# A hybrid encoder trunk with experts: the scatter of expert rows in column groups of the array

## The chip, the cores and the metric

The kernel runs on one core of a Trainium2 chip. Times are device microseconds (us) of one execution, and the median of several runs is compared. TensorE, VectorE, ScalarE, GpSimd and SyncE are the engines; SBUF is the working memory of 128 partitions, and PSUM is the memory that TensorE writes, eight banks of 128 partitions by 512 fp32 numbers. A matmul takes a stationary operand (loaded into the array by a weight load, up to 128 rows by 128 columns) and streams a moving operand of up to 512 columns through it; the stationary operand's columns become partitions of the result.

## What is computed

A trunk of two layers works on 256 tokens of width 1024. Each layer has a mixer (windowed attention beside a short convolution) and a feed-forward part: a dense SwiGLU in the first layer, and in the second a choice of 2 of 8 experts for each token. The reference, cut to the part around the change:

```python
def moe_swiglu(h, w_router, w_gate, w_up, w_down):
    t = h.reshape(b * s, d)
    logits = (t @ w_router).astype(jnp.float32)
    top_val, top_idx = lax.top_k(logits, TOP_K)
    gates = jax.nn.softmax(top_val, axis=-1)
    combine = jnp.sum(jax.nn.one_hot(top_idx, N_EXPERTS, dtype=jnp.float32) * gates[..., None], axis=1)
    out = jnp.zeros_like(t)
    for e in range(N_EXPERTS):
        out = out + combine[:, e:e + 1].astype(t.dtype) * swiglu(t, w_gate[e], w_up[e], w_down[e])
    return out.reshape(b, s, d)
```

## The kernel before

All weights come from HBM in fp32. ScalarE rounds a piece of 128 by 1024 weights to the matmul's fast fp32 format (line 425, `hi`), VectorE forms the rest (line 825, `lo`), and TensorE multiplies in three products, hi·hi, lo·hi and hi·lo (lines 1359 to 1361, `three`), each 128 by 512 columns. A ring of six pieces (`RING`) connects the three engines; the semaphore `lo_done` counts pieces that are ready, `piece_used` those that TensorE has finished. SyncE issues the weight transfers, each as soon as `lo_done` shows that its buffer is free.

In the expert layer TensorE runs `experts()` (line 1587). For each of the 8 experts in turn it works on a tile of up to 128 tokens: `gather` (line 1606) picks the expert's tokens from `xn` with a 0/1 matrix `sel`; `gu` computes gate and up in halves of 256 columns; `turn` transposes the gated rows; `down` accumulates the down projection in PSUM banks 3 and 4. The loop of `one_tile` (line 1639) does this for 14 halves. An expert with more than 128 tokens takes `two_tiles` (line 1665), with both tiles side by side. The plan for this (`code`) is computed on the chip, and here one expert of the eight, the last, takes two tiles.

The result of expert p−1 is added to the tokens while expert p has begun. ScalarE and VectorE copy banks 3 and 4 to `y`, 128 expert rows by 1024 (`rows_out`). `scatter_last` (line 1624) waits for both copies and for `gselT`, the 128-by-256 matrix that holds a row's gate weight at the column of its token, and calls `scatter` (line 1615). That makes four products: for each half t of the tokens and each half c of the width, `gselT` columns of t (128) are stationary and `y` columns of c (512) moving, all in plain fp32. Each lands in a bank of its own, 5, 6, 7 and 5 again; the last waits until the bank is free. Each product increments `scattered`, and VectorE then adds the bank to `x` (`add_rows`, line 1191; the addition is line 1199) and increments `x_changed`.

What follows on TensorE: in `one_tile` `clear` (line 1508) zeroes banks 3 and 4 with two matmuls of zeros, and `gu(1)` goes on with 24 matmuls, before `turn(0)` needs `gate(0)`, which VectorE does after the additions. In `two_tiles` the scatter is split (`r1=2`, `r0=2`, lines 1691 and 1693) around `gu_both`, and TensorE waits for all additions (`x_changed`, line 1696) before it clears. The second tile has a scatter of its own at line 1718, ahead of the next gather. A last scatter (line 1735) follows the loop; VectorE's additions, the final norm and the store come after it. Other places where TensorE uses less than the whole array are the scores of attention (line 1389), with 64 rows: heads 0 to 3 lie in rows 0 to 63 and heads 4 to 7 in rows 64 to 127. The router (line 1566) has a stationary operand of 16 columns.

Of the kernel before, what the change touches and what calls it, by code (L numbers as in the profile page):

```python
# [33 lines left out]
P = 128  # L34
# [60 lines left out]
def build_trunk(nc, x_d, pos_d, mix_g, w_in, conv_w, sink, att_g, conv_g, w_out, ffn_g, dg, du, dd,  # L95
                router, eg, eu, ed, final_g, out_d):
    ctx = ExitStack()
    with ctx:
        def sb(name, shape, dt=F32):
            return ctx.enter_context(nc.sbuf_tensor(name, shape, dt))  # L100
# [4 lines left out]
        bank = [ctx.enter_context(nc.psum_tensor(f"bank{i}", [P, 512], F32)) for i in range(8)]  # L105
# [14 lines left out]
        y = sb("y", [P, D])  # L120
# [5 lines left out]
        gselT = sb("gselT", [P, SEQ])  # L126
# [1211 lines left out]
        def _(pe):  # L1338
            mm, tr = nc.tensor.matmul, nc.tensor.transpose
# [247 lines left out]
            def experts():  # L1587
# [27 lines left out]
                def scatter(p, added, done, banks=(5, 6, 7, 5), r0=0, r1=4):  # L1615

                    for r in range(r0, r1):
                        t, c, b = r // 2, r % 2, banks[r]
                        if b in banks[:r]:
                            pe.wait_ge(added, p)  # L1620
                        mm(bank[b][:, :], gselT[:, t * P:(t + 1) * P], y[:, c * 512:(c + 1) * 512],  # L1621
                           start=True, stop=True).then_inc(done, 1)

                def scatter_last(p, banks=(5, 6, 7, 5), r0=0, r1=4):

                    if r0 == 0:
                        pe.wait_ge(y_act, p + 1)
                        pe.wait_ge(y_dve, p + 1)
                        pe.wait_ge(gselT_out, p + 1)
                    scatter(12 + 4 * p + 1, x_changed, scattered, banks, r0, r1)  # L1630
# [34 lines left out]
                def two_tiles(p, first, n0, u):  # L1665
# [50 lines left out]
                    pe.wait_ge(y2_dve, u + 1)  # L1716
                    pe.wait_ge(gselT2_out, u + 1)
                    scatter(4 * u + 1, x_changed2, scattered2, (0, 1, 2, 7))
                    gather(p + 2)
                    pe.wait_ge(x_changed2, 4 * u + 4)  # L1720
# [43 lines left out]
```

## Time and profile before

| what | value |
|---|---|
| median of 3 runs | 1656.64 us (1655.93 to 1657.57) |
| span of the profiled execution, first to last instruction | 1653.7 us |
| its total with what lies around the span | not given; the median is 2.9 us above the span |
| TensorE, matmuls | busy 1590.2 us, 96% |
| TensorE, weight loads (beside the matmuls) | busy 1306.2 us, 79% |
| VectorE | busy 1177.2 us, 71% |
| ScalarE | busy 986.1 us, 60% |
| mean granted TensorE clock | 0.987 |

In the profile PE is TensorE's matmuls, PEld its weight loads, DVE VectorE, ACT ScalarE. A duration of a matmul is its latency: successive matmuls overlap, so a stream is read by the distance of its starts. In a timeline row the columns are the start in us from the span's start, the time to the end of the group in us, engine, line, operation, operands (output <- inputs), the stationary operand's rows*columns, the moving operand's partitions by columns, and the number of instructions (x). What stands in brackets is the idle time ahead and who ended it. The granted clock is a share of 2.4 GHz.

### The profile page before, as it was taken

The page shows a single profiled execution, that of the slowest core. Times are in us where ns is not written, and L with a number is a line of the kernel's source. Part 1 is how long each engine was busy: PE and PEld are TensorE (multiplying, and loading weights), DVE is VectorE, ACT ScalarE, POOL GpSimd, SP SyncE. Part 2 cuts the span into 40 slices and gives each one's busy share as a digit, 9 for nine tenths or more (in the row PEclk, how much of TensorE's full clock was granted, in tenths as well). Part 3 has the DMA queues.
Part 4 walks back from the last instruction along what each step waited for, and adds up shares of the span by engine and source line. Part 5 has one row for each costly group of instructions (what it writes and reads, how often), then busy time and mean ns, then how long its engine had stood idle before and what let it go on. Part 6 is the DMA issues. An engine that isn't in the chain of part 4 may idle for free.

```text
span 1653.7 us, 22917 instructions
## 1 busy us (share of the span) xinstructions
PE 1590.2 (96%) x7170; PEld 1306.2 (79%) x7170; DVE 1177.2 (71%) x1467; ACT 986.1 (60%) x1335; POOL 9.8 (1%) x33
## 2 busy tenths in 40 slices
PE   7989999898799999999999999999999998999996
PEld 6777888787678878878878878878887887788874
DVE  5754545557589799789979979979979974645443
ACT  6544434454467587677767767767767753434342
POOL 2000000000000000000000000000000000000000
PEclk9999999999899999999999999999999999999999
DMA  9344463320779979979979979979988992644500
GB/s 346 125 154 153 180 225 119 138 102 2 267 298 382 351 269 382 351 270 389 344 267 388 347 268 393 341 289 373 385 307 309 383 350 92 237 152 155 194 6 26
DMA packets 177794, 417.89 MB, mean 253 GB/s; under 512 B 4144, under 2 KB 8272, under 8 KB 177760
## 3 DMA queue, kind: packets, MB, share of 16 engines
q1 hardware_dynamic: 176400, 415.25, 67.5%
q0 software_dynamic: 512, 1.12, 0.2%
q10 hardware_dynamic: 848, 1.06, 0.2%
q8 instruction: 22, 0.36, 0.1%
q14 instruction: 12, 0.10, 0.0%
HBM read 416.36 MB, written 1.05 MB: 252 GB/s over the span
## 4 chain that ended last, share of the span: by engine, by line
PE 90%; DVE 6%; ACT 3%; issue 1%; DMA 0%; DVEq 0%; ACTq 0%
PE bank L1359 27%; PE bank L1361 26%; PE bank L1360 26%; PE bank L1611 5%; PE bank L1621 2%; DVE lo L825 1%; PE bank L1599 1%; ACT raw_d L485 1%; ACT act_hi L425 1%; DVE mx L914 1%; DVE raw_d L911 1%; PE bank L1468 0%; PE bank L1409 0%; DVE act_lo L849 0%; PE bank L1680 0%
## 5 line engine op out<-in xcount | busy, mean ns | idle before, releaser
L825 DVE TENSOR_TENSOR lo<-raw_gu,hi 128x1024 fp32r<-128x1024 f32 x544 | 631.3, 1220 | 34.3 <-ACT hi L425 32.8
L1359 PE MATMUL bank<-hi,act_hi 128*128 128x512 f32 (+1 forms) x1408 | 559.2, 397 | 18.2 <-DVE lo L825 6.6
L425 ACT ACTIVATE hi<-raw_gu 128x1024 fp32r (+1 forms) x544 | 542.9, 1055 | 43.7 <-PE bank L1361 32.5
L1361 PE MATMUL bank<-hi,act_lo 128*128 128x512 f32 (+1 forms) x1408 | 548.4, 390 | 0.0
L1360 PE MATMUL bank<-lo,act_hi 128*128 128x512 f32 (+1 forms) x1408 | 548.4, 389 | 0.0
L825 DVE TENSOR_TENSOR lo<-raw_d,hi 128x1024 fp32r<-128x1024 f32 x246 | 290.5, 1223 | 57.4 <-ACT hi L425 56.8
L1359 PEld LDWEIGHTS bank<-hi,act_hi 128*128 128x128 f32 x1408 | 266.4, 189 | 74.1 <-issue 13.6
L1361 PEld LDWEIGHTS bank<-hi,act_lo 128*128 128x128 f32 x1408 | 266.2, 189 | 55.5
L1360 PEld LDWEIGHTS bank<-lo,act_hi 128*128 128x128 f32 x1408 | 266.9, 190 | 50.9
L425 ACT ACTIVATE hi<-raw_d 128x1024 fp32r (+1 forms) x246 | 247.0, 1056 | 0.0
L1359 PE MATMUL bank<-hi,at_hi 128*128 128x512 f32 x592 | 232.4, 393 | 11.4 <-DVE lo L825 5.9
L1361 PE MATMUL bank<-hi,at_lo 128*128 128x512 f32 x592 | 231.0, 390 | 0.0
L1360 PE MATMUL bank<-lo,at_hi 128*128 128x512 f32 x592 | 230.4, 389 | 0.0
L425 ACT ACTIVATE at_hi<-bank 128x256 fp32r<-128x256 f32 (+1 forms) x123 | 52.8, 429 | 229.7 <-PE bank L1599 191.3
L1359 PEld LDWEIGHTS bank<-hi,at_hi 128*128 128x128 f32 x592 | 111.1, 188 | 37.9 <-DVE lo L825 8.8
L1361 PEld LDWEIGHTS bank<-hi,at_lo 128*128 128x128 f32 x592 | 111.1, 188 | 23.4
L1360 PEld LDWEIGHTS bank<-lo,at_hi 128*128 128x128 f32 x592 | 111.2, 188 | 22.6
L1244 DVE TENSOR_TENSOR gated<-silu,bank 128x256 f32<-128x256 f32 x28 | 10.5, 418 | 109.5 <-ACT silu L707 109.5
L1611 PE MATMUL bank<-sel,xn 128*128 128x128 f32 x320 | 77.7, 404 | 1.1 <-DVE sel L1156 1.1
L1611 PEld LDWEIGHTS bank<-sel,xn 128*128 128x128 f32 x320 | 77.0, 334 | 1.5 <-issue 1.4
L707 ACT ACTIVATE silu<-bank 128x256 f32<-128x256 f32 x28 | 9.2, 382 | 111.4 <-PE bank L1361 111.4
L1177 DVE TENSOR_TENSOR at_lo<-bank,at_hi 128x256 fp32r<-128x256 f32 x98 | 41.6, 424 | 42.9 <-ACT at_hi L425 39.4
(202 smaller groups left out, 727.7 us busy)
## 6 DMA issues: line engine op xcount, KB each, us to landing
raw_gu<-in_moe_w_gate SPq DMA_DIRECT2D x56, 2048.0 KB, 9.4
raw_gu<-in_moe_w_up SPq DMA_DIRECT2D x56, 2048.0 KB, 14.2
raw_d<-in_moe_w_down SPq DMA_DIRECT2D x56, 2048.0 KB, 16.3
raw_gu<-in_w_in SPq DMA_DIRECT2D x7, 2048.0 KB, 13.1
raw_gu<-in_dense_w_gate SPq DMA_DIRECT2D x5, 2048.0 KB, 8.0
raw_gu<-in_dense_w_up SPq DMA_DIRECT2D x5, 2048.0 KB, 12.9
raw_d<-in_dense_w_down SPq DMA_DIRECT2D x5, 2048.0 KB, 15.4
raw_gu<-in_w_out SPq DMA_DIRECT2D x8, 1024.0 KB, 9.6
```

The lines of the kernel that those rows point to most:

```text
L425: return nc.scalar.activation(out, in_, ACT.Copy, **kw)
L485: nc.scalar.activation(prob[:, h * 256:(h + 1) * 256], prob[:, h * 256:(h + 1) * 256], ACT.Exp, bias=nmx[:, t, h:h + 1], accum_out=psums[: ...
L825: v.tensor_tensor(out, src, h, ALU.subtract).then_inc(lo_done, 1)
L911: link(v.scalar_tensor_tensor(out=two_heads, in0=bank[b][:, :].rearrange("p (h n) -> p h n", h=2), scalar=HD ** -0.5, in1=mask[:, t, :].un ...
L914: ins = v.tensor_reduce(mx[:, 2 * b:2 * b + 2], two_heads, AX, ALU.max)
L1177: v.tensor_tensor(at_lo[:, c], bank[2][:, c], at_hi[:, c], ALU.subtract).then_inc(atTl_done, 1)
L1359: mm(out, ah, wh, start=start, stop=False, **kw)
L1360: mm(out, ah, wl, start=False, stop=False, **kw)
L1361: return mm(out, al, wh, start=False, stop=stop, **kw)
L1599: ins = tr(bank[2][:, c:c + P], gated[:, half, i * P:(i + 1) * P], ident[:, :])
L1611: ins = mm(bank[5 + k // 4][:, (k % 4) * P:(k % 4 + 1) * P], xn[:, t, k:D:KT], sel[:, t, :], start=t == 0, stop=t == 1)
L1621: mm(bank[b][:, :], gselT[:, t * P:(t + 1) * P], y[:, c * 512:(c + 1) * 512], start=True, stop=True).then_inc(done, 1)
```

## The change

`scatter` issues each product in parts: for t = 0 two matmuls with 64 stationary columns each, written to partitions 0 to 63 and 64 to 127 of the bank; for t = 1 four with 32 columns each, written to four quarters of the partitions. All parts of a product stream the same 512 columns of `y`. The increment is on the last part. The callers, waits and semaphore counts stay.

```diff
--- before.py
+++ after.py
@@ -1618,8 +1618,12 @@
                         t, c, b = r // 2, r % 2, banks[r]
                         if b in banks[:r]:
                             pe.wait_ge(added, p)
-                        mm(bank[b][:, :], gselT[:, t * P:(t + 1) * P], y[:, c * 512:(c + 1) * 512],
-                           start=True, stop=True).then_inc(done, 1)
+                        wide = 64 if t == 0 else 32
+                        for g in range(P // wide):
+                            m = slice(g * wide, (g + 1) * wide)
+                            ins = mm(bank[b][m, :], gselT[:, t * P + g * wide:t * P + (g + 1) * wide],
+                                     y[:, c * 512:(c + 1) * 512], start=True, stop=True)
+                        ins.then_inc(done, 1)
 
                 def scatter_last(p, banks=(5, 6, 7, 5), r0=0, r1=4):
 
```

## Rows read from the trace of the kernel before

**Rows 1.** The page: span, engines, the chain that ended last.

```profile
span 1653.7 us, 22917 instructions
...
PE 1590.2 (96%) x7170; PEld 1306.2 (79%) x7170; DVE 1177.2 (71%) x1467; ACT 986.1 (60%) x1335; POOL 9.8 (1%) x33
...
PE 90%; DVE 6%; ACT 3%; issue 1%; DMA 0%; DVEq 0%; ACTq 0%
...
PE bank L1359 27%; PE bank L1361 26%; PE bank L1360 26%; PE bank L1611 5%; PE bank L1621 2%; DVE lo L825 1%; PE bank L1599 1%; ACT raw_d L485 1%; ACT act_hi L425 1%; DVE mx L914 1%; DVE raw_d L911 1%; PE bank L1468 0%; PE bank L1409 0%; DVE act_lo L849 0%; PE bank L1680 0%
```

**Rows 2.** Windows over three expert periods: length, PE, PEld, DVE, ACT, POOL busy, clock.

```profile
830.90:961.60 130.70, 129.86 (x578) 106.63 (x578) 112.56 (x125) 94.97 (x118) 0.00 (x0) 1.00 0.90 336
...
1092.30:1223.00 130.70, 129.86 (x578) 106.63 (x578) 112.57 (x125) 94.98 (x118) 0.00 (x0) 1.00 0.90 337
```

**Rows 3.** The chain in one period, longest pieces: start, us, what.

```profile
961.60 7.63 PE bank L1611 x32
...
981.78 3.43 PE bank L1621 x8
```

**Rows 4.** Timeline, first scatter: start, us, engine, line, operation.

```profile
458.56 0.39 PE L1361 MATMUL bank<-hi,act_lo 128*128 128x512 f32 x1
458.79 3.59 PE L1621 MATMUL bank<-y,gselT 128*128 128x512 f32 x8
461.82 1.03 PE L1511 MATMUL bank<-zeros 128*128 128x512 f32 x2
462.68 0.39 PE L1359 MATMUL bank<-hi,act_hi 128*128 128x512 f32 x1
...
460.93 0.19 PEld L1621 LDWEIGHTS bank<-y,gselT 128*128 128x128 f32 x1 [0.24 <-issue]
```

**Rows 5.** Line 1621: durations in ns (min/median/max), first and last start.

```profile
L1621 PE MATMUL bank<-y,gselT x80: 590/592/1193, 458.8 to 1645.6; 128*128 128x512 f32 x80
```

**Rows 6.** Timeline, two-tile expert: the split scatter and the clear behind it.

```profile
1390.55 1.88 PE L1621 MATMUL bank<-y,gselT 128*128 128x512 f32 x4
...
1404.68 1.88 PE L1621 MATMUL bank<-y,gselT 128*128 128x512 f32 x4
...
1407.65 0.98 PE L1511 MATMUL bank<-zeros 128*128 128x512 f32 x3 [0.66 <-DVE x L1199]
```

**Rows 7.** Timeline, the second tile's scatter and the last; window with the clock.

```profile
1626.41 3.67 PE L1621 MATMUL bank<-y,gselT 128*128 128x512 f32 x8 [0.83 <-ACT y L425]
...
1641.13 5.09 PE L1621 MATMUL bank<-y,gselT 128*128 128x512 f32 x8 [3.34 <-DVE y L1189]
...
1641.13:1643.80 2.67, 2.67 (x3) 0.50 0.00 0
```

**Rows 8.** Timeline, attention scores on 64 rows and neighbours; their durations in ns.

```profile
47.90 0.39 PE L1361 MATMUL bank<-hi,act_lo 128*128 128x512 f32 x1
48.22 2.96 PE L1389 MATMUL bank<-raw_d 64*128 64x256 f32 x16
51.11 0.50 PE L1359 MATMUL bank<-hi,act_hi 128*128 128x512 f32 x1
...
51.45 0.40 PE L1360 MATMUL bank<-lo,act_hi 128*128 128x512 f32 x1
...
50.37 0.81 PE L1389 MATMUL bank<-raw_d 64*128 64x256 f32 x3
...
373.19 1.10 PE L1389 MATMUL bank<-raw_d 64*128 64x256 f32 x4 [0.41 <-DVE raw_d L928]
...
L1389 PE MATMUL bank<-raw_d x64: 376/376/480, 48.2 to 375.8; 64*128 64x256 f32 x64
```

**Rows 9.** Timeline, weight loads of the values product, and durations of line 1409.

```profile
389.84 3.65 PEld L1409 LDWEIGHTS bank<-raw_d 128*128 128x128 f32 x32
...
L1409 PEld LDWEIGHTS bank<-raw_d x128: 186/192/192, 74.9 to 393.3; 128*128 128x128 f32 x128
```

**Rows 10.** Line 1566 (router), weight loads of 16 columns.

```profile
L1566 PEld LDWEIGHTS bank<-act_hi,rout_hl x8: 92/93/93, 429.5 to 432.1; 128*16 128x16 f32 x8
```

## The prediction

> **What bounds the kernel now.** I began with the page. TensorE is busy 96% of the span and carries 90% of the chain that ended last; line 1621, the scatter that is edited, has 2% of that chain [rows 1]. The next question was whether the experts, where the line runs, are as full as the average. Three expert periods of 130.70 us each, cut at the gather, show TensorE busy for 129.86 us in every one, at full clock, with VectorE at 112.57 us and ScalarE at 94.98 us [rows 2]. So TensorE is the bound there, and a microsecond added to its queue is a microsecond of the kernel unless it falls into the 0.84 us a period that TensorE is idle. The chain of such a period has the gather and the scatter as its longest pieces, the scatter's 3.43 us in full [rows 3].
>
> Then the scatter itself. One fp32 matmul of the program is two matmul instructions in the trace: 4 calls are x8, 3.43 us, 0.429 us each, with weight loads of 0.19 us beside them that never delay one; the matmuls before and after follow without a gap [rows 4]. Ten scatters make the x80 of the line [rows 5]: seven in the one-tile experts (first and last at 458.95 and 1243.18), one in the two-tile expert, split by `r1=2` and `r0=2` into two fours with gate and up pieces between [rows 6], one more for its second tile, behind an idle of 0.83 us, and the last of all, which follows an idle of 3.34 us and takes 5.09 us, with a granted clock of 0.50, the lower level of 1.2 GHz, over its first 2.67 us [rows 7].
>
> **The change.** It keeps what is computed and takes the 128 token columns of a call as 2 groups of 64 (t = 0) or 4 groups of 32 (t = 1). Each group streams the same 512 columns of `y`. Of 40 calls, 20 become 2 and 20 become 4: 80 matmul instructions become 20·2·2 + 20·4·2 = 240, and as many weight loads. No wait, DMA or semaphore count changes; the increment sits on the last group's matmul, so VectorE's additions (line 1199) are released at a call's end as now. What decides is what 240 instructions cost on the array. There are three terms.
>
> *Streaming.* If groups run side by side, a call still lasts two slots of 0.429 us and the term is 0. If they run one behind the other, it is 160 extra instructions at 0.429 us = 68.6 us. Line 1621 can't say which, but the attention scores can: they use 64 rows of the array, heads 0 to 3 the lower, heads 4 to 7 the upper half. A lone stream of them has its starts 0.217 us apart ((0.81 − 0.376) / 2, 376 ns being the duration of one) [rows 8]. Sixteen in one line would last 15·0.217 + 0.10 (the late second start, below) + 0.376 = 3.73 us; the row says 2.96 [rows 8]. Four slots less 0.1 are missing, so two streams did run at once, at full rate each. Those are row halves, not column groups, but it is the nearest row there is, and I take 0, with 68.6 as the other end.
>
> *Switching the split.* The last whole-array matmul starts at 47.90, the first half-array one at 48.22, 0.32 us later where 0.23 is the rule; another time the first four take 1.10 us to the fourth's end, so the second came 1.10 − 0.376 − 2·0.217 = 0.29 us behind the first, where 0.217 is the rule. On the way back 50.81 (last start, 50.37 + 2·0.217) to 51.11 is 0.30 for 0.217, and 51.11 to 51.45 is 0.34 for 0.23 [rows 8]. Each switch thus costs 0.09 us before its first matmul and about 0.1 behind it: 0.19. I read it as the array running empty and then waiting for a weight load that is hidden otherwise. The edit makes three switches in a scatter (128 to 64, 64 to 32, 32 to 128), four where it is split in two, and only one that counts in the last (64 to 32). 7·3 + 4 + 3 + 1 = 29 switches, 5.5 us. Bounds: 0, should column groups need no emptying, and 29·0.2 = 5.8.
>
> *Getting the groups started.* The second group of 64 can start only when three loads are in (its own is the third), the fourth of 32 when seven are; the groups end staggered by as much, and the next split waits for the last. That is 2 and 6 loads more than the first needs. Where loads are the limit (the 128-by-64 products of attention, 32 in 3.65 us) one of 128 columns comes every 0.112 us [rows 9]. Scaled by width, 0.056 and 0.028, it is 2·0.056 + 6·0.028 = 0.28 us a scatter; 16-column loads took 93 ns where 128-column ones took 186 to 192, so width does matter [rows 9, 10]. Against it, a narrower first load exposes 0.06 and 0.08 less than the 0.1 above. Net 0.14, times ten: 1.4 us. Bounds: −1.3 (no stagger), and with loads at 0.112 whatever their width 9 us, plus 8·0.112 − 0.857 = 0.04 for each of 20 calls: 10 us.
>
> What hides nothing: ScalarE and VectorE get the delay as slack, as TensorE hardly waits for them here; the additions of the one-tile case have the 24 matmuls of `gu(1)` behind them, 24·0.227 = 5.4 us, before `gate(0)` is wanted. In the two-tile case TensorE already waits 0.66 us for the addition at line 1199 before it clears [rows 6]; a later scatter moves that wait, it does not absorb it. Behind the last scatter stand only additions, the final norm and the store, all in line. The expert DMAs are prefetched against `lo_done` and see nothing.
>
> The sum is 0 + 5.5 + 1.4 = 6.9 us. The profiled span of 1653.7 us becomes 1660.6. The page gives no total for that execution; the median of the runs, 1656.64, lies 2.9 us above its span, and I carry the difference: **1663.6 us**, with an own range of 1660 to 1672 from the bounds of the second and third terms.
>
> **A rule weighed against the trace.** By FIFO, the scores above would save one slot only, where head 4 follows head 3, and their row would read 3.5 us, not 2.96 [rows 8]; so matmuls of the upper half must have begun ahead of earlier ones of the lower. The Trainium skill (TensorE: Matmul & The Clock Gate, "Part 3: Packing small matmuls — row/col tiling") says that matmuls keep program order in start and end without exception. By that rule, the trace disagrees, and the sum would be that of the second rival. The same section measured three column tiles at 2.38 times one's rate, which speaks against the third rival; no row here shows column groups.
>
> **Rivals.**
> 1. *Not slower.* Column groups share the rows through which `y` streams, so the change of width may need no emptying, and the queue runs through all three widths without a step. Then only the stagger is left, between −1.3 and +2.8 us with the narrow loads, and the kernel lies at 1655.5 to 1659.5, likeliest 1656.6. It decides if a switch costs under 0.07 us, since 29 of them are then 2 us. Against it: the switch of the scores costs 0.19 on the way in and on the way back [rows 8]. Chance 0.13.
> 2. *Groups start in program order.* Each group is a pair (high part, low part) that must follow itself, so its second instruction pairs only with the next group's first. Two calls of two groups are 8 instructions in 5 slots for 4, two of four groups 16 in 9 for 4: six slots of 0.429, 2.6 us a scatter, 25.7 us in all. With the switches 1656.6 + 25.7 + 5.5 = 1688. For it: a fixed order is the simplest machine. Against it: rows 8, as far as halves of rows speak for groups of columns. Chance 0.12.
> 3. *The change does not do what it says.* The narrow operands are run with the array whole, or the groups queue for the one stream of `y`, which row halves do not share (each half reads its own partitions, here all four groups read the same ones). 68.6 us, with or without switches: 1725 to 1731. Chance 0.10.
>
> **How the numbers follow.** The forecast (side by side, switches paid) has 0.62, a remainder of 0.03 goes to what I don't see. About 0.2%, 3.3 us, is what a measurement of this kernel can tell from no change; the forecast's range begins at 3.4, so nearly all of it is slower, and rival 1 is "same". Faster 0.03, same 0.13, slower 0.84. The range takes the forecast, rival 1 and rival 2 and leaves rival 3 and the remainder out: 1656 to 1689.
>
> **What would show it.** In the changed profile line 1621 has x240 matmuls. If the forecast holds, the one-tile scatter takes some 4.1 us from its first matmul to the clear for 3.43 now, the clear comes about 0.3 us behind the last group's start where 0.43 would be a slot, four starts of a 32-wide call fall within about 0.2 us, and the expert period grows from 130.70 to about 131.4 us. A period of 133.9 is rival 2, one of 138 rival 3, one of 130.7 to 130.9 rival 1. I am wrong if starts of different groups stand a full 0.429 us apart, if the loads come more slowly than 0.1 us each, or if the period grows by more than the scatter does, as that would be an engine I took to have slack.

## The result and the profile after

The changed kernel took 1663.01 us (median of 4 runs, 1661.44 to 1663.58), the kernel before 1656.29 us beside it (4 runs, 1655.27 to 1657.57): a ratio of 1.0040, 95% interval 1.0027 to 1.0052, 6.7 us more. 1663.6 had been forecast. The profiled execution is the one of 1661.44 us, with a span of 1659.7 us, 6.0 us over that of before. The total is close, and the way to it is not the one predicted, so the profile after is read in some detail.

From the page after, the lines that answer to [rows 1]:

```profile
span 1659.7 us, 23237 instructions
PE 1596.8 (96%) x7330; PEld 1299.0 (78%) x7330; DVE 1177.5 (71%) x1467; ACT 985.8 (59%) x1335; POOL 9.8 (1%) x33
```

160 more matmuls and as many loads, as counted. Busy time of the matmuls grows by 6.6 us only, since groups that run side by side are not counted twice. Line 1621 is now line 1624; its entry (durations in ns, first and last start, forms) gives:

```profile
L1624 PEld LDWEIGHTS bank<-y,gselT x240: 106/110/231, 458.8 to 1651.2; 128*32 128x32 f32 x80, 128*64 128x64 f32 x40
L1624 PE MATMUL bank<-y,gselT x240: 592/592/1061, 458.8 to 1651.6; 128*32 128x512 f32 x80, 128*64 128x512 f32 x40
```

The count is x240; the forms at the end list only a part of it. A matmul of a narrow group has the same median of 592 ns as one of the whole array [rows 5]. The timeline of the first scatter, matmuls:

```profile
458.51 0.39 PE L1361 MATMUL bank<-hi,act_lo 128*128 128x512 f32 x1
458.83 3.79 PE L1624 MATMUL bank<-y,gselT 128*64 128x512 f32 x24
462.55 0.73 PE L1511 MATMUL bank<-zeros 128*128 128x512 f32 x2
463.12 0.40 PE L1359 MATMUL bank<-hi,act_hi 128*128 128x512 f32 x1
```

and the loads of the same stretch:

```profile
458.83 0.20 PEld L1624 LDWEIGHTS bank<-y,gselT 128*64 128x64 f32 x4 [0.35 <-issue]
459.31 0.14 PEld L1624 LDWEIGHTS bank<-y,gselT 128*64 128x64 f32 x2 [0.29 <-issue]
459.74 0.14 PEld L1624 LDWEIGHTS bank<-y,gselT 128*64 128x64 f32 x2 [0.29 <-issue]
460.69 0.16 PEld L1624 LDWEIGHTS bank<-y,gselT 128*32 128x32 f32 x8 [0.81 <-issue]
461.15 0.13 PEld L1624 LDWEIGHTS bank<-y,gselT 128*32 128x32 f32 x4 [0.30 <-issue]
461.58 0.13 PEld L1624 LDWEIGHTS bank<-y,gselT 128*32 128x32 f32 x4 [0.30 <-issue]
462.55 0.30 PEld L1511 LDWEIGHTS bank<-zeros 128*128 128x128 f32 x2 [0.84 <-issue]
```

Two matmuls stand in the first slot, by a narrower window of the same timeline:

```profile
458.83 0.65 PE L1624 MATMUL bank<-y,gselT 128*64 128x512 f32 x2
```

The loads tell the order best (an fp32 matmul of the program is two instructions, a high and a low part, each with its load). At 458.83 four loads go out within 0.2 us (two groups, two parts each), then two at a time every 0.43 us; at 460.69 eight within 0.16 us, which is one load's 0.11 and 0.05 more, then four at a time every 0.43 us. So all groups of a call run together, slot by slot. The changes of width are the gaps: from the last whole-array product to the first group, 458.51 to 458.83, it is 0.32 us where 0.23 is the distance without a change. The 64-wide slots of 0.43 us begin at 458.83, 459.31 (0.05 late: the load of this slot is exposed, which means that TensorE waits for it) and 459.74, the fourth by that at 460.17, to end at 460.60; the 32-wide loads come at 460.69, 0.09 late. From the last product ahead to the first behind the clear it is 4.61 us (458.51 to 463.12), where it was 4.12 (458.56 to 462.68 [rows 4]): **0.49 us a scatter**, for 0.71 forecast.

The expert period, though, grew by more. These are the scatter's pieces in the chain that ended last, in the kernel after, one period apart each:

```profile
590.36 3.72 PE bank L1624 x24
721.78 3.72 PE bank L1624 x24
853.23 3.72 PE bank L1624 x24
```

131.42 and 131.45 us, and 131.42 to 131.46 over all six, for 130.70: 0.74 more, so 0.25 us a period lies outside the scatter. Nearly all of it (0.24) is in the loop over the halves of an expert. The transposes at line 1599 end each half of an iteration; before, then after:

```profile
535.46 0.38 PE L1599 MATMUL bank<-ident,gated 128*128 128x128 f32 x2
...
569.12 0.38 PE L1599 MATMUL bank<-ident,gated 128*128 128x128 f32 x2
```

```profile
536.05 0.38 PE L1599 MATMUL bank<-ident,gated 128*128 128x128 f32 x2
...
569.78 0.38 PE L1599 MATMUL bank<-ident,gated 128*128 128x128 f32 x2
```

Two iterations take 33.66 us before and 33.73 after: 16.83 and 16.87 each, six an expert, 0.24 us. The loss sits in the first ten or so products behind the transposes: nine distances in a row take 2.09 us (544.93 to 547.02) where they took 2.06 (544.33 to 546.39), and the later ones in the half keep their 0.227. No engine is waited for there.

The two-tile expert lost nothing. Its lines after, for [rows 6]:

```profile
1395.85 1.94 PE L1624 MATMUL bank<-y,gselT 128*64 128x512 f32 x8
1410.01 1.92 PE L1624 MATMUL bank<-y,gselT 128*32 128x512 f32 x16
1411.87 0.66 PE L1684 MATMUL bank<-ident,gated 128*128 128x128 f32 x4
1412.89 1.20 PE L1511 MATMUL bank<-zeros 128*128 128x512 f32 x4 [0.36 <-DVE x L1199]
```

From the first half scatter to the clear it is 17.04 us for 17.10. The first half is followed by a wait for VectorE's gates (line 1244), which shrank from 1.26 to 1.11 us. Behind the second half, TensorE's wait for VectorE's additions shrank from 0.66 to 0.36 us, because VectorE's own work ahead of them sets their time: its timeline in the kernel after shows that it begins its gates 5.24 us later than before (1410.89 for 1405.65), as far as everything had slid by then, and adds right behind them:

```profile
1410.89 0.75 DVE L1244 TENSOR_TENSOR gated<-silu,bank 128x256 f32<-128x256 f32 x2 [8.26 <-ACT silu L707]
1411.56 1.28 DVE L1199 TENSOR_TENSOR x<-x,bank 128x512 f32<-128x512 f32 x2
```

The last two scatters, for [rows 7]:

```profile
1631.62 3.79 PE L1624 MATMUL bank<-y,gselT 128*64 128x512 f32 x24 [0.83 <-ACT y L425]
1635.34 7.89 PE L1611 MATMUL bank<-sel,xn 128*128 128x128 f32 x32
1643.07 0.38 PE L1640 MATMUL bank<-ident,gsel 128*128 128x128 f32 x2
1646.78 5.43 PE L1624 MATMUL bank<-y,gselT 128*64 128x512 f32 x24 [3.34 <-DVE y L1189]
```

Behind the first of these stands the gather (line 1611). Its first two matmuls, before and then after:

```profile
1629.92 0.51 PE L1611 MATMUL bank<-sel,xn 128*128 128x128 f32 x2
```

```profile
1635.34 0.74 PE L1611 MATMUL bank<-sel,xn 128*128 128x128 f32 x2
```

The second starts 0.23 us later than it did, and the gather as a whole takes 7.73 us to the transposes behind it for 7.49. So nearly all of the 0.24 us stands at this one place, and it fits a load that the change back to 128 columns exposes: the load at 1635.34 begins with the gather's first matmul and takes 0.31 us, where before the loads ran ahead. Those at lines 1511 and 1359 take 0.19, so that more is exposed here.

The last scatter takes 5.43 us for 5.09, but this is not the price of its one change of width. It comes behind an idle and runs in good part at the lower granted clock (0.50 over its first 2.67 us before [rows 7], 0.57 over its first 3.99 us after), and the moments when the clock falls and rises differ from run to run. The scatter that no edit touched takes 5.09 us in the profile before, 5.12 in e7, 5.26 in e6 and 5.37 in e11 and e12 (kernels of the next section); the changed one takes 5.43 here and 6.68 in e10, where the granted clock is 0.50 over the first 5.97 us of it.

The account of the 6.0 us of the span, by starts in the two traces: seven one-tile scatters 3.4; the loops and what lies between, up to the two-tile expert, 1.9; the two-tile expert −0.1; the second tile's scatter, and the gather behind it, 0.4; the last scatter 0.3, clock included. Each is rounded.

### The profile page after: what moved, and what is told of

It is laid out like the page before. It is cut to its first block, busy times and chain, and to the rows that moved or that the text cites. A ratio compares the mean times of both kernels' runs of the same rounds, so it can differ in the third digit from the quotient of the medians.

```text
span 1659.7 us, 23237 instructions
## 1 busy us (share of the span) xinstructions
PE 1596.8 (96%) x7330; PEld 1299.0 (78%) x7330; DVE 1177.5 (71%) x1467; ACT 985.8 (59%) x1335; POOL 9.8 (1%) x33
## 4 chain that ended last, share of the span: by engine, by line
PE 90%; DVE 6%; ACT 3%; issue 1%; DMA 0%; DVEq 0%; ACTq 0%
PE bank L1359 27%; PE bank L1361 26%; PE bank L1360 26%; PE bank L1611 5%; PE bank L1624 2%; DVE lo L825 1%; PE bank L1599 1%; ACT raw_d L485 1%; ACT act_hi L425 1%; DVE mx L914 1%; DVE raw_d L911 1%; PE bank L1468 0%; PE bank L1409 0%; DVE act_lo L849 0%; PE bank L1511 0%
```

## The experiments

The views used are the same in all: the distance of the scatters in the chain (period), the timeline from the last product ahead of the scatter to the first behind the clear (scatter), and the distance of the transposes (loop, the time of one iteration, two halves). All numbers are of the one-tile experts. "over before" is against 4.12 us for the scatter.

| kernel | scatter over before, us | period, us | loop, us | ratio to before, 95% |
|---|---|---|---|---|
| before | 0 | 130.70 | 16.83 | |
| the change (64, 64, 32, 32) | 0.49 | 131.44 | 16.87 | 1.0040 (1.0027 to 1.0052) |
| e1 all 64 | 0.35 | 131.30 | 16.87 | 1.0043 (1.0026 to 1.0060) |
| e2 all 32 | 0.34 | 131.06 | 16.83 | 1.0014 (1.0005 to 1.0024) |
| e3 alternating | 0.78 | 131.50 | 16.83 | 1.0045 (1.0029 to 1.0062) |
| e4 one group | 7.33 | 138.07 | 16.83 | one run, 1730.6 us |
| e5 group first | 1.37 | 132.13 | 16.83 | one run, 1669.7 us |
| e6 before, delayed | 0.46 | 131.17 | 16.83 | one run, 1659.4 us |
| e7 before, dead code | 0 | 130.70 | 16.83 | 0.9998 (0.9988 to 1.0007) |
| e8 change, dead code | 0.49 | 131.45 | 16.87 | 1.0033 (1.0020 to 1.0045) |
| e9 change, delayed 0.46 | 0.95 | 131.90 | 16.87 | one run, 1666.2 us |
| e10 change, delayed 0.23 | 0.72 | 131.67 | 16.87 | one run, 1666.7 us |
| e11 before, delayed 0.35 | 0.35 | 131.07 | 16.83 | one run, 1658.5 us |
| e12 before, delayed 0.49 | 0.49 | 131.33 | 16.83 | one run, 1661.2 us |

Where a period has grown by more than scatter and six loops account for (0.14 us in e12), the rest lies in the products between the clear and the first transposes. Single periods agree to 0.05 us, kernel totals to a microsecond or more: the first scatter of these traces starts anywhere from 458.2 to 461.2 us, whatever the kernel, and the last takes more or less of the lower clock, so a difference of totals is only read where several runs stand behind it. (That is why e10's 1666.7 us stand over e9's 1666.2, with periods 0.23 us shorter.)

### What the width costs: e1, e2, e3

```diff
-                        wide = 64 if t == 0 else 32
+                        wide = 64                          # e1
+                        wide = 32                          # e2
+                        wide = 64 if c == 0 else 32        # e3
```

> All four products of a scatter in two groups of 64. The change's own scatter took 0.49 us more than the one before, from the last matmul ahead of it to the second clear, and its period 131.43 us for 130.70. Theory (groups run side by side, only changes of width cost, 0.09 us to run empty plus the exposed load: 0.05 for 64 columns, 0.03 for 32, 0.11 for 128): two changes of width, 0.09 + 0.05 + 0.09 + 0.11 + 0.01 for the second group's start = 0.35 us a scatter over before, period 130.70 + 0.35 = 131.05, or 131.29 if the 0.24 us a period that the change shows outside its scatter come again. Rival (groups take part of each other's time, by number of groups): fewer parts than the change's two and four, so clearly under 0.35, or 64 columns show slots over 0.43 us.

> All four products in four groups of 32: 16 parts where the change has 12. Theory: two changes of width, 0.09 + 0.03 + 0.09 + 0.11 + 0.02 = 0.34 us a scatter over before, so less than the change's 0.49 in spite of more instructions; period 131.04, or 131.28 with the 0.24 us outside the scatter. Rival (the number of parts costs): more than the change, over 0.49 us a scatter and a period over 131.45.

> The same parts as in the change, but the widths alternate with the half of the width c: 64, 32, 64, 32. Theory: five changes of width for three, 0.14 + 0.12 + 0.14 + 0.12 + 0.20 and 0.06 for the groups' starts = 0.77 us a scatter over before, 0.29 more than the change; period 131.72 if the 0.24 us outside are there, 131.48 if not. Rival (the number of parts costs, not the changes): 0.49 us and 131.43, as the change.

The timelines of the first scatter of e2 (4.47 us from the first row's start to the last's) and e3 (4.90), for 4.12 before:

```profile
459.77 0.39 PE L1361 MATMUL bank<-hi,act_lo 128*128 128x512 f32 x1
460.09 3.64 PE L1624 MATMUL bank<-y,gselT 128*32 128x512 f32 x32
...
464.24 0.39 PE L1359 MATMUL bank<-hi,act_hi 128*128 128x512 f32 x1
```

```profile
460.76 0.39 PE L1361 MATMUL bank<-hi,act_lo 128*128 128x512 f32 x1
461.08 4.08 PE L1624 MATMUL bank<-y,gselT 128*64 128x512 f32 x24
...
465.66 0.39 PE L1359 MATMUL bank<-hi,act_hi 128*128 128x512 f32 x1
```

All three came where the theory put them: 0.35, 0.34 and 0.78 for 0.35, 0.34 and 0.77. Its constants had been read from the trace of the change, the three sums had not. 32 matmul instructions cost no more than 16; the same 24 cost 0.49 with three changes of width and 0.78 with five. Within 0.01 us the number of parts costs nothing beyond the few hundredths for starting the groups, and the changes of width cost the rest. e2, with two changes and the loop at 16.83 us, is the best of the column-group kernels (ratio 1.0014, interval 1.0005 to 1.0024), and it is still slower than the kernel before: no run of this case shows anything that the groups give back.

### What the separate groups save: e4

```diff
-                            m = slice(g * wide, (g + 1) * wide)
+                            m = slice(0, wide)
```

> Every part of a product is written to the first 64 or 32 partitions, so that all of them use one column group; the other partitions' rows are left out of the result. Theory (it is the separate groups that make the parts free): the parts stand in one line, 24 instructions at 0.43 us = 10.3 us for a scatter where the change takes 3.2 + 0.4, period 130.70 + 6.9 + about 0.5 = 138.1 us, the kernel about 75 us slower than before. Rival (the narrow array is simply faster per part, by less to stream or to drain): less than 0.43 us from start to start, period well under 138.

The timeline of its first scatter:

```profile
459.92 0.39 PE L1361 MATMUL bank<-hi,act_lo 128*128 128x512 f32 x1
460.24 10.63 PE L1624 MATMUL bank<-y,gselT 128*64 128x512 f32 x24
...
471.37 0.40 PE L1359 MATMUL bank<-hi,act_hi 128*128 128x512 f32 x1
```

11.45 us for 4.12, 7.33 more; the period grew by 7.37 where 7.4 was expected, and the kernel took 1730.6 us, 74 over before. The same number of instructions in one group, with most rows of the result left out, stand in line at 0.43 us each. That is the price of the third rival, and the separate groups are what saves it.

### How far ahead the groups are started: e5

```diff
+                    for t in range(r0 // 2, r1 // 2):
+                        wide = 64 if t == 0 else 32
                         for g in range(P // wide):
                             m = slice(g * wide, (g + 1) * wide)
+                            for c in range(2):
+                                b = banks[2 * t + c]
+                                if g == 0 and b in banks[:2 * t + c]:
+                                    pe.wait_ge(added, p)
...
```

> For t = 1 the parts are issued group by group, both halves of the width for one group before the next group; the same 12 parts and three changes of width as the change. The trace of the scores fits a queue in which only four matmuls may wait unstarted, each starting as soon as its own part of the array is free. By that rule 16 instructions in the order of the groups take 7 slots of 0.43 us for 4: 1.29 us more a scatter than the change, period 132.7. If loads were taken strictly in order with one waiting load for each group it would be 10 slots, 2.57 us more, period 134.0. If the queue were deep, nothing: 131.43.

The period was 132.13 us, none of the three. The loads of its 32-wide part:

```profile
462.07 0.14 PEld L1625 LDWEIGHTS bank<-y,gselT 128*32 128x32 f32 x2 [0.81 <-issue]
462.92 0.17 PEld L1625 LDWEIGHTS bank<-y,gselT 128*32 128x32 f32 x8 [0.72 <-DVE x L1199]
463.38 0.14 PEld L1625 LDWEIGHTS bank<-y,gselT 128*32 128x32 f32 x3 [0.29 <-issue]
463.81 0.14 PEld L1625 LDWEIGHTS bank<-y,gselT 128*32 128x32 f32 x3 [0.29 <-issue]
```

The edit had brought forward a wait I had counted as satisfied: bank 5 serves the first and the fourth product, and in this order the wait for bank 5 stands right behind the first group of the third product, and holds back the other three groups too, until VectorE's addition is done (0.72 us without a load, put down to line 1199). Group one runs alone until then, two slots; then all four groups start within 0.06 us and need four slots. Two slots more, 0.86 us, is the 0.88 over the change that was measured. In that burst the fourth group's first matmul started past seven older ones that had to wait (the second part of the fourth product's first group, three each of groups two and three), so a queue in which only four may wait, as I had read it from the scores, is out. With the wait in the way, the run does not show what group order alone costs. Why the upper heads of the scores start 1 us late is open (below).

### Where the 0.24 us of the loop comes from: e6 to e12

There were three ideas: a delay of TensorE at this place, the place of its program in memory, and the narrow array itself.

```diff
 # e6 (before) and e9 (change): behind scatter_last(p) in one_tile
                     clear((3, 4))
+                    clear((3, 4))
 # e10 (change): clear((3,)) instead; e11, e12 (before): clear((3,)) or clear((3, 4)), and
+                    mm(bank[3][:, 0:256], zeros[:, 0:P], zeros[:, 0:256], start=True, stop=True)  # e12: 0:32
 # e7 (before) and e8 (change): at the head of two_tiles, never taken here
+                    with pe.If(u > 1):
+                        for _ in range(24):
+                            mm(bank[3][:, 0:P], gsel[:, 0, :], ident[:, :], start=True, stop=True)
```

> The kernel before, with clear((3, 4)) done twice in the one-tile experts: two more matmuls of zeros, a delay of TensorE of 2 x 0.227 = 0.45 us in the place and of the size of the change's own. It asks where the 0.24 us a period outside the scatter come from. If any delay of TensorE there shifts it against the other engines so that its matmuls run a little slower, the period is 130.70 + 0.45 + 0.24 = 131.39. If it is the narrow array or the place of TensorE's program in memory, 131.15.

> The kernel before, with 24 more fp32 products in TensorE's program, as many as the change adds, ahead of the one-tile loop but behind a branch that is never taken with these inputs; nothing of them is executed. If the place of the program in memory sets how fast TensorE is fed behind its waits, the one-tile period grows by about 0.24 us to 130.94 with the scatter as before. If not, it stays 130.70.

> The changed kernel with the same 24 products behind the branch that is never taken. If the place of the program matters, the period differs from the change's 131.43 by some 0.1 to 0.3 us either way, with the scatter the same 0.49 us over before. If the 0.24 us outside the scatter belong to the narrow array, it stays 131.43.

The chains of e6 and e7, two scatters each:

```profile
590.56 3.43 PE bank L1621 x8
721.73 3.43 PE bank L1621 x8
```

```profile
592.04 3.43 PE bank L1621 x8
722.73 3.43 PE bank L1621 x8
```

131.17 and 130.69 us, and 131.45 for e8: a delay of 0.46 alone does not bring the longer loop, 24 products of dead code neither bring it to the kernel before nor take it from the change. Both ideas fall in this form. For the place of the program e3 and e4 say more than the dead code: they issue exactly as many instructions as the change, in the same places of the code, so what follows stands where it does in the change, and both have the shorter loop. Nor is it the narrow array as such: e2, e3, e4 and e5 have it in every scatter and keep 16.83. So the last four runs asked whether the moment of entry decides.

> The changed kernel with clear((3, 4)) done twice in the one-tile experts, 0.455 us more. The loop behind the scatter was found at either of two lengths, 16.83 us an iteration (before, all 32, alternating, one group, group first, the delayed one before) or 16.87 us (the change, all 64, the change with dead code), six iterations an expert. If the longer one belongs to the narrow array in the change's order, the period is 131.43 + 0.455 = 131.89. If it only hangs on when TensorE enters the loop, another entry gives the shorter one with about four chances in five, by the count so far: 131.64.

> The changed kernel with one more matmul of zeros, 0.227 us, in the same place. Period 131.66 if the loop stays at 16.87 us, 131.42 if it falls back to 16.83 us. Only the entry's time differs from the run with two more.

> The kernel before, no narrow array at all, with one matmul of zeros of 512 columns and one of 256 more: about 0.35 us, the delay of all 64, which had the longer loop. If the entry's time decides and is met closely enough, the loop is 16.87 us and the period 130.70 + 0.35 + 0.24 = 131.29; if the narrow array is needed for it, 16.83 us and 131.05.

> The kernel before with two matmuls of zeros of 512 columns and one of 32 more: about 0.49 us, the delay of the change. Same question: 131.43 with the longer loop, 131.19 with the shorter one. A longer loop in either of these two would show that it needs no narrow array; the shorter one in both leaves it open.

The chains of e9 and e11:

```profile
591.33 3.72 PE bank L1624 x24
723.23 3.72 PE bank L1624 x24
```

```profile
590.06 3.43 PE bank L1621 x8
721.12 3.43 PE bank L1621 x8
```

e9 (131.90) and e10 (131.67) kept the longer loop with the entry moved by 0.46 and 0.23 us. e11's clear was over 0.35 us late, as e1's, and it had the shorter one. e12's clear was over as late as the change's (0.49), but its matmul of 32 columns cost more behind it:

```profile
463.05 0.18 PE L1645 MATMUL bank<-zeros 128*128 128x32 f32 x1
463.07 0.48 PE L1359 MATMUL bank<-hi,act_hi 128*128 128x512 f32 x1
463.39 0.40 PE L1360 MATMUL bank<-lo,act_hi 128*128 128x512 f32 x1
```

The first product takes 0.48 us and the second starts 0.32 us behind it where 0.23 is usual. From the last product ahead of the scatter to the transposes it is 10.18 us (458.47 to 468.65) where it was 9.57 (458.56 to 468.13), so TensorE came to the loop 0.61 us late, and e12 did not meet the change's delay there; its loop is the shorter one too. Sorted by how late the clear is over, the shorter loop stands at 0, 0.34, 0.35, 0.46, 0.49, 0.78, 1.37 and 7.33 us and the longer at 0.35, 0.49, 0.72 and 0.95. No simple order by the moment of entry parts them; a dependence on differences of 0.02 us or less is not excluded. All the kernels with the longer loop (the change, e1, e8, e9, e10) issue both products of t = 0 in two groups of 64, call by call, and then t = 1 call by call; but so does e4, except that its parts share one group. What picks the loop's length is **not settled**.

## Why the prediction was right, and where not

*Streaming, 0 us.* Right. The scores of the kernel before, on halves of the rows, were a fair guide to groups of columns: two slots a call with two groups and with four, and e4 shows what it would have cost otherwise: 7.33 − 0.49 = 6.84 us a scatter, for the 6.86 in the 68.6.

*A change of width, 0.19 us.* The mechanism held, and e1 to e3 priced it: 0.09 us without a matmul, each way and at each width, which I read as the array running empty, then the exposed load, 0.05 for 64 columns, 0.03 for 32 and 0.11 for 128. The forecast's 0.19 is the one for 128 columns (0.20), and its correction for narrow loads (0.14 a scatter) was the right size. At the gather, whose loads are longer, the second start is 0.23 late, twice the 0.1 of the forecast for the load. The first rival, without the emptying, is out.

*The groups' start, 0.28 us a scatter.* This term was mis-sized, by nearly ten times. I had let the loads follow one another at a pace scaled from the 0.112 us of whole-array loads [rows 9]. Loads of different groups go in together, like their matmuls: eight in 0.16 us with their own 0.11 in it. The term measures 0.03 us a scatter.

*29 switches and nothing absorbed.* 24 counted: the four of the split scatter did not, nor did the one into the second tile's scatter, which follows an idle. In the two-tile expert I wrote that a later scatter "moves that wait, it does not absorb it". It does absorb it: the additions wait behind VectorE's gates, which hang on ScalarE and not on the scatter, and the wait at the clear went from 0.66 to 0.36 us. The switch of the last scatter can't be priced: with the clock as it was, an unchanged one differs by 0.28 us between runs (5.09 to 5.37), and that its 0.34 meets the forecast of 0.33 is luck.

*Other engines have slack.* True of waits. But of the marks I had set for being wrong, one came true: the period grew by 0.74 and the scatter by 0.49. The scatters alone come to 3.4 − 0.1 + 0.4 + 0.3 = 4.0 us, for 6.9 forecast; 1.9 us from the loops, which nothing in the prediction held, fills most of the gap. So the total of 1663.0 for 1663.6, and the period of 131.44 for "about 131.4", are right by luck in part: terms too large met a loss not foreseen.

*The other signs.* From its first matmul to the clear the scatter takes 3.72 us (458.83 to 462.55), not 4.1. The clear comes a slot and 0.09 us behind the last group's start, not 0.3 us behind it; the last slot is run out in full before the width changes. The range of 1660 to 1672 given with the sum does not follow from its bounds at the lower end (0 for the switches and −1.3 for the starts give 1655.3); the final range of 1656 to 1689 does not hang on it.

*Program order.* The second rival is out. The second group's first load, and its matmul, go with the first group's first, ahead of the first group's second: four loads at 458.83 and then two by two. 24 instructions that paired only in program order would have made the period 133.9 us. The Trainium skill (TensorE: Matmul & The Clock Gate, "Part 3: Packing small matmuls — row/col tiling") has matmuls start and end in program order; the trace disagrees, for column groups (four loads and two matmuls in the first slot) as for row halves [rows 8].

## What to carry to other kernels

Splitting a stationary operand that fills the array into column groups gained nothing in any of these kernels: every group streams the same moving columns, and the groups side by side take the same slots that the whole array took. If narrow groups are needed anyway, keep one width through a stretch: the parts are all but free, each change of width cost 0.12 to 0.20 us on a TensorE that is never idle (0.32 in front of a product with longer loads, 0.09 + 0.23), and nothing where it waited soon after. And compare the growth of the edited stretch with that of the period around it before a matching total is taken for a confirmed mechanism.

## What the runs showed that I had not expected

- Loads of different column groups overlap: eight loads of 106 to 109 ns within 0.16 us.
- The matmuls of different groups overtake each other by at least seven places of the queue (e5). In the scores of the kernel before, by the starts in the trace, the upper heads begin only 0.97 us after the lower ones. Eight matmuls and eight loads of the lower heads lie between in the program, which would fit a pace of 0.06 us an instruction (an estimate, 0.97 / 16); no run tested it.
- One and the same loop of 16.83 us runs at 16.87 us in five of fourteen kernels, stable over all its iterations and over two delays, with VectorE and ScalarE starting at the same places behind the transposes to a few ns until TensorE's own 22 ns carry them on. Its cause is open.
- A matmul of zeros with 32 moving columns added 0.16 us to the period (e12's 131.33 over e6's 131.17), far above its share of a 512-column one's 0.227. Only 0.03 of it shows before the next start; the rest is in the products behind it. It fits a next load of 0.19 us that 32 columns don't hide; no run varied this.
